# Experts' weights of a mixture of experts: the order of the down and up loads in SP's queue

## The reference

```
group = argmax(t @ wg + bg)                       # 1 of 4 groups
top_val, top_idx = top_k(e_sel, 2)                # 2 of the group's 8 experts
for gi in range(4):
    hid = silu(einsum('td,edf->tef', t, w1[gi])) * einsum('td,edf->tef', t, w3[gi])
    hid = hid * gate[:, gi, :, None]
    y = y + einsum('tef,efd->td', hid, w2[gi])
```

## Time and profile before

| | us |
|---|---|
| median of 3 runs | 1742.28 |
| profiled execution, its own time | 1748.31 |
| its span | 1746.5 |
| TensorE busy | 1576.9 (90% of the span) |
| VectorE busy | 833.4 (48%) |
| ScalarE busy | 421.8 (24%) |
| GpSimd busy | 164.9 (9%) |
| SP's own queue of loads (q1) | 282.76 MB, 41.2% of 16 DMA engines' span |

### The profile page before, as it was taken

The page is one execution under the profiler, slowest core; times in us unless marked ns, Lnnn a source line. Parts: engine busy times, 40 slices in busy tenths (PEclk is TensorE's granted clock), DMA queues, the critical chain, the costliest instruction groups (busy, mean ns, idle before and its releaser), DMA issues.

```text
span 1746.5 us, 28216 instructions
## 1 busy us (share of the span) xinstructions
PE 1576.9 (90%) x12141; PEld 954.4 (55%) x12141; DVE 833.4 (48%) x1428; ACT 421.8 (24%) x836; POOL 164.9 (9%) x185
## 2 busy tenths in 40 slices
PE   6999989998799999879887899999999996988877
PEld 2885478887464685444333368845558544333332
DVE  7551856664385625444222174446643554431225
ACT  2114245554300222211000031017511312100002
POOL 2000133330000000011111100000000001110101
PEclk9999989999799999979999899999999997998998
DMA  7028100000531511269999952220025024999995
GB/s 242 1 97 288 42 4 4 4 5 4 217 126 67 221 68 52 99 233 414 424 425 424 372 197 96 89 86 19 2 75 198 20 105 156 389 423 425 424 420 209
DMA packets 81503, 312.89 MB, mean 179 GB/s; under 512 B 17776, under 2 KB 18856, under 8 KB 56608
## 3 DMA queue, kind: packets, MB, share of 16 engines
q1 hardware_dynamic: 69280, 282.76, 41.2%
q0 software_dynamic: 10944, 24.10, 3.8%
q10 hardware_dynamic: 1152, 4.19, 0.6%
HBM read 305.81 MB, written 33.29 MB: 194 GB/s over the span
## 4 chain that ended last, share of the span: by engine, by line
PE 73%; issue 7%; DVE 5%; ACT 3%; DMA 0%; POOL 0%; PEld 0%; DVEq 0%; ACTq 0%; POOLq 0%
PE PS L2489 15%; PE PS L617 13%; PE PS L750 10%; PE PS L1282 7%; PE PS L2514 7%; PE PS L1616 2%; PE PS L574 2%; PE PS L2474 2%; PE PS L2438 2%; PE PS L588 2%; PE PS L1592 1%; PE PS L1864 1%; PE PS L1885 1%; PE PS L1875 1%; PE PS L2032 1%
## 5 line engine op out<-in xcount | busy, mean ns | idle before, releaser
L750 PE MATMUL PS<-arena,ring 128*128 128x256 f32 x1152 | 251.2, 379 | 0.1
L750 PEld LDWEIGHTS PS<-arena,ring 128*128 128x128 f32 x1152 | 218.4, 190 | 31.2 <-issue 1.4
L2489 PE MATMUL PS<-ring,arena 128*64 128x512 f32 x512 | 137.4, 698 | 51.4 <-issue 48.3
L617 PE MATMUL PS<-ring,arena 128*128 128x512 f32 x400 | 178.1, 596 | 0.7 <-ACT arena L1830 0.7
L2497 DVE TENSOR_TENSOR arena<-PS,arena 128x256 f32<-128x256 f32 x32 | 13.6, 424 | 256.3 <-PE PS L2504 235.4
L2489 PE MATMUL PS<-arena 128*64 128x512 f32 x512 | 120.6, 626 | 12.9 <-issue 10.1
L617 PEld LDWEIGHTS PS<-ring,arena 128*128 128x128 f32 x400 | 75.5, 192 | 89.0 <-issue 88.0
L2489 PEld LDWEIGHTS PS<-ring,arena 128*64 128x64 f32 x512 | 44.8, 160 | 141.9 <-issue 137.9
L2494 ACT ACTIVATE arena<-PS 128x256 f32<-128x256 f32 x32 | 12.3, 383 | 363.0 <-PE PS L2489 363.0
L2489 PEld LDWEIGHTS PS<-arena 128*64 128x64 f32 x512 | 41.8, 144 | 90.1 <-issue 86.5
L574 PE MATMUL PS<-arena,ring 128*128 128x512 f32 (+1 forms) x256 | 84.7, 493 | 0.0
(11 more groups left out here) (329 smaller groups left out, 2387.3 us busy)
## 6 DMA issues: line engine op xcount, KB each, us to landing
arena<-in_moe_w SPq DMA_DIRECT2D x96, 1024.0 KB, 9.8
ring<-in_moe_w SPq DMA_DIRECT2D x96, 1024.0 KB
ring<-in_sb_wqkv SPq DMA_DIRECT2D x6, 2048.0 KB, 8.4
ring<-in_xa_wkv SPq DMA_DIRECT2D x4, 2048.0 KB, 15.9
ring<-in_xa_wq SPq DMA_DIRECT2D x4, 2048.0 KB, 8.5
ring<-in_xa_wo SPq DMA_DIRECT2D x4, 2048.0 KB, 14.4
h<-in_x SPq DMA_DIRECT2D x8, 512.0 KB, 5.4
ring<-in_rw_wr SPq DMA_DIRECT2D x2, 2048.0 KB, 14.2
```

What stands on the lines that cost most here:

```text
L617: ins = pe.matmul(PS[:, BANK_OF[g], :], rows(k), cols[:, k, :], start=(k == 0 and not grows), stop=(k == 3), skip_group_check=grows)
L750: ins = pe.matmul(PS[:, BANK_OF[g], M * c:M * c + M], rows[:, k, o:o + P], cols[:, k, :], start=(c + k == 0 and not grows), stop=(k == 3), ...
L2489: ins = pe.matmul(bank(2, 2, F)[r, :, :], xgT[p][:, k, r], w[a][:, :, k, :], start=(k == 0), stop=(k == KC - 1))
```

## The change

In the loop over n the two calls change places. For each n from 4 on, the down weights of pair n are now issued ahead of the up weights of pair n+1. The waits inside the two helpers stay as they are.

```diff
             for n in range(4, NPE):
+                down_weights(n)
                 if n + 1 < NPE:
                     up_weights(n + 1)
-                down_weights(n)
```

## The result

The changed kernel takes 1778.79 us, the median of 4 executions (1775.56 to 1785.43); the kernel before took 1741.72 beside it. The ratio is 1.021, 95% interval 1.0185 to 1.0236. So the change costs some 37 to 39 us; I had forecast 23.4 and a range up to 1777. The way was right, the size was not.

The account below looks back on a forecast made before the run. The DMA stream of weights bounds both expert loops, through the landing of pair 15's up weights. Layer 0: 5.35 + 3.1 + 3 = 11.5; layer 1: 11.9; together 23.4 us on 1742.28, giving 1765.7 us, range 1753 to 1777.

Parts of the forecast that it names:

- What bounds the kernel: Expert loops of both layers: DMA is at its limit; each loop ends with pair 15's up weights landing plus a tail.
- First step: Each expert loop: one down group goes ahead of every up group, a shift taken once, 5.35 us per layer.
- Second step: Start of each expert loop: pair 5's up weights are issued later, the stream runs dry; 3.1 and 3.5 us.
- The rule I had put beside it: Every transfer: fixed 2 us, mostly after the last byte; no gap would be absorbed, sum 2.0 us larger.
- Third step: Later pairs of each loop: stream runs dry where TensorE's wait is under the 1.6 us restart; 3 us per layer.
- A: Expert loops: engine spread swallows the gap and waits settle, only the order costs; 10.7 to 13.7 us, chance 0.15.
- B: Expert loops: longer waits bring the low clock, every one of 9 pairs pays 1.6 us; 45 us, 1787, chance 0.11.
- C: Expert loops: not slower, if the stream ran faster and a pair landed in 15.3 us instead of 16.3; chance 0.07.

Follow-up runs that it names:

- e6: Kernel before, with the second half of each down projection's contraction left out and all loads kept; -1 us against before, ratio 0.9996.
- e3: Kernel before, with the two calls swapped at n = 14 only (pair 14's down weights ahead of pair 15's up weights); +14 us, ratio 1.0082.
- e1: Changed kernel's order kept, but a third down buffer lets all up weights be issued as early as before; +8 us against before, ratio 1.0044.
- e4: Kernel before, with the two calls swapped at n = 4 only (pair 4's down weights ahead of pair 5's up weights); +9 us, ratio 1.0049.
- e2: Kernel before, old order, but SP waits for pair n-2's down projection before issuing pair n+1's up weights; +4 us, ratio 1.0023.
- e5: Changed kernel, with the second half of each down projection's contraction left out and all loads kept; +23 us against before, ratio 1.0131.

## Why the prediction was right or wrong, by its steps

*What bounds the kernel.* Right. e6 takes work from TensorE in every pair and gains nothing; what moves the landing of the last up group moves the time, as e3 shows with a single swap.

*First step, the order.* Right: 5.35 us per layer; e1 shows 4.8 and 5.0, and e3's growth of 5.9 and 6.9 less its gaps of 1.3 and 2.2 gives 4.6 and 4.7, all within the scatter of the readings.

*Second step, the gap at the start.* Right: 3.1 and 3.5 us were taken out of bounds of 1.3 to 4.5; e4 shows 3.5 and 3.9, e2 3.8 and 3.7 at pair 15. Pair 6 was forecast 8.45 and 8.85 us later and came 9.4 and 9.0 later. Less the order's 5.35 that is 4.0 and 3.6. The rows of q1 above show that the engines do end one after another, as I had supposed, and yet little of a gap is absorbed: 5.1 us are lost between 806 and 816 in layer 0, 1.0 more than the 4.1 worked out, and 4.0 reach pair 6. The rule I had put beside it (the Trainium skill, DMA: Bandwidth & Descriptors, anatomy of one DMA: a fixed 2 us, most of it after the last byte) is given in that section for the DMAs that GpSimd issues, and these are SyncE's. The gaps of 4.1 and 4.5 us without absorption, which I had tied to it, are no nearer to what came than my reduced ones: layer 0 is nearer to the first, layer 1 to the second. And the trace does not show 2 us after the last byte: q1 still has a share of 27.3% in 878.5:879, about 1 us before TensorE starts at 879.71.

*Third step, the slack in steady state.* This one failed, and with it the sum. I wrote: "Where that wait is shorter than the 1.6 us restart, the stream runs dry for the difference", and priced it at 3 us per layer with 0 and 14 as bounds. It was 9.1 and 8.4 us in the first profile, 11.0 and 10.5 in the second, beyond the 6 us that I had named as the sign of being wrong in this step. The mechanism was right: the dips stand where it put them, every second pair, with the short waits. The threshold was wrong. TensorE's wait ends with the landing, after the last of the 16 engines is done, and most of them have run dry well before it; I had worked out that lag, 2.8 us, one step earlier, and used it only as something that might save time. The stream is dry from there on, so to a first approach the gap is restart plus lag less the wait. In layer 0 the five intervals after a short wait grew from 84.2 to 95.5 us in sum, 2.3 us each, the four others shrank by 2.2 us in sum: net 9.1. With a mean short wait of 1.15 us, 2.3 = 1.6 + lag - 1.15 gives a lag of 1.8 us. The transfer missing around each of the ten short waits of the two layers, counted in the same way as for e3 (1.4 to 2.9 us behind waits of 0.53 to 2.44) gives 1.3 to 3.0, and e3's two gaps 1.5 and 1.5. In layer 1 two of these dips stand behind waits of 1.98 and 2.44 us, where my threshold allowed none. The lag is no constant, and e5 shows that its formula misses the shallow dips behind long waits. With a lag of 2 in the third step the four short waits of the earlier trace rows would have given 1.6 + 2 less 1.18, 0.70, 1.26 and 0.48, that is 10.8 us per layer, and a sum of 39 us instead of 23.4. That is hindsight, with a lag taken from the result; it agrees so well partly by luck, since it puts the third step 1.7 to 2.4 us too high and leaves the second 0.1 to 0.9 too low against the first profile.

*The rivals.* A (only the order costs) is excluded by e4 and by the growth. B had a neighbouring price, 45 us (1787, nearer to the 1778.79 measured than my forecast of 1765.7), for another reason: it let every pair pay and had the low clock as its driver. The low clock plays no such part: the ups after the long waits run 8.4 to 9.3 us in layer 0 after the change, no longer than before. Where B was right is in that long and short waits go on alternating and do not settle, which my own sum had taken from the row's numbers and then priced too low. C (not slower) found nothing in its favour.

*The range.* It ended at 1777, between the forecast and B, and the median is 1778.79. With the third step's own upper bound of 14 us in both layers, which I had worked out, it would have reached 1788.

## What to carry to other kernels

When a stream of loads is the bound, ask what is still queued behind the transfer that the compute waits for at the moment when the next loads are issued. Here 1 MB behind it took away nine tenths of the growth, and nothing behind it cost 2.3 us every second pair. The slack to compare with is the restart plus the time over which the engines run dry ahead of the landing, about 3.4 us by the landings here, and not the restart alone. Even that is no safe bound: e5 still lost transfer behind waits of 4 to 5 us. And a swap of two calls in a queue that waits is two changes, of the order and of the issue times: make each alone, and then both, because their costs need not add.

## What the runs showed that I had not expected

Late issue with the old order costs 4 us, and the new order with early issue 8 us, but the two together 37 to 39. The start of the expert loop moves by up to 7.6 us between executions over the same instructions, in a kernel whose whole time repeats to 0.2% in some sets and to 1% in others; reading a loop against its own first pair removes most of that, down to some 2 us. And the end of the kernel has a second chain, store, wait, eight gathers on GpSimd, within some 3 us of the first.
